# Hybrid decoder layer on one core: the b/a logits with both weight halves in one stationary block, and two banks of activations turned per job

## The reference, cut to what matters

```python
h = rms_norm(x, norm1_g[l])
proj = h @ w_in[l]
qkv_g, z, b_logit, a_logit, q_s, k_s, v_s, gate_logits = jnp.split(proj, split_points, axis=-1)
...
beta = jax.nn.sigmoid(b_logit)
g = -jnp.exp(a_log) * jax.nn.softplus(a_logit + dt_bias)
...
x = x + (g_gdn * y_gdn + g_swa * y_swa) @ w_out[l]
h = rms_norm(x, norm2_g[l])
x = x + jnp.square(jax.nn.relu(h @ w_ff_up[l])) @ w_ff_down[l]
return rms_norm(x, final_norm_g)
```

## Time and profile before

| | before |
|---|---|
| median of 3 runs | 1839.65 us (1839.18 to 1839.65) |
| profiled execution | 1839.5 us |
| its span, first to last instruction | 1837.7 us |
| PE busy | 1818.1 us, 99% of the span, 10928 matmuls |
| PEld busy | 1479.4 us, 81% |
| DVE busy | 1086.0 us, 59% |
| ACT busy | 883.4 us, 48% |
| POOL busy | 115.4 us, 6% |
| DMA, mean over the span | 172 GB/s |

### The profile page before, as it was taken

The page is one execution under the profiler, slowest core; times in us unless marked ns, Lnnn a source line. Parts: engine busy times, 40 slices in busy tenths (PEclk is TensorE's granted clock), DMA queues, the critical chain, the costliest instruction groups (busy, mean ns, idle before and its releaser), DMA issues.

```text
span 1837.7 us, 29585 instructions
## 1 busy us (share of the span) xinstructions
PE 1818.1 (99%) x10928; PEld 1479.4 (81%) x10928; DVE 1086.0 (59%) x1531; ACT 883.4 (48%) x1388; POOL 115.4 (6%) x82
## 2 busy tenths in 40 slices
PE   7999999999999999999999999999999999999998
PEld 6888787787787877778888888888888888888886
DVE  5567686777766576665555555555544455555454
ACT  6464454554644555555444455444433344444443
POOL 0022031040220000000000000000000000000110
PEclk9999999999999999999999999999999999999999
DMA  6543443434434544445656655555555555555554
GB/s 252 173 160 124 142 145 120 150 127 139 149 127 139 182 152 152 151 158 161 205 194 200 206 199 189 188 185 183 193 192 193 192 192 184 185 187 187 194 195 138
DMA packets 88020, 316.33 MB, mean 172 GB/s; under 512 B 9712, under 2 KB 10224, under 8 KB 87792
## 3 DMA queue, kind: packets, MB, share of 16 engines
q1 hardware_dynamic: 87056, 312.58, 50.9%
q0 software_dynamic: 576, 2.10, 0.3%
q10 hardware_dynamic: 288, 0.18, 0.1%
HBM read 312.72 MB, written 2.10 MB: 171 GB/s over the span
## 4 chain that ended last, share of the span: by engine, by line
PE 98%; DVE 0%; issue 0%; DMA 0%; ACT 0%; DVEq 0%; POOLq 0%; POOL 0%; SPq 0%; ACTq 0%
PE acc L325 30%; PE acc L326 29%; PE acc L327 29%; PE J L382 2%; PE J L421 1%; PE J L531 1%; PE J L413 1%; PE J L580 1%; PE J L591 1%; PE J L425 1%; PE J L389 1%; PE J L370 1%; PE J L544 1%; PE J L451 0%; PE J L554 0%
## 5 line engine op out<-in xcount | busy, mean ns | idle before, releaser
L1159 DVE TENSOR_TENSOR w_lo<-raw,w_hi 128x1024 fp32r<-128x1024 f32 x584 | 715.7, 1231 | 506.8 <-ACT w_hi L780 506.1
L780 ACT ACTIVATE w_hi<-raw 128x1024 fp32r<-128x1024 f32 x584 | 617.0, 1060 | 605.4 <-PE acc L327 602.7
L325 PE MATMUL acc<-w_hi,hT_hi 128*128 128x512 f32 x1440 | 579.8, 403 | 5.8 <-DVE hT_lo L1177 4.2
L326 PE MATMUL acc<-w_lo,hT_hi 128*128 128x512 f32 x1440 | 562.8, 391 | 0.0
L327 PE MATMUL acc<-w_hi,hT_lo 128*128 128x512 f32 x1440 | 562.3, 391 | 0.0
L325 PEld LDWEIGHTS acc<-w_hi,hT_hi 128*128 128x128 f32 x1440 | 270.8, 188 | 72.7 <-issue 11.2
L327 PEld LDWEIGHTS acc<-w_hi,hT_lo 128*128 128x128 f32 x1440 | 270.9, 188 | 58.1
L326 PEld LDWEIGHTS acc<-w_lo,hT_hi 128*128 128x128 f32 x1440 | 271.3, 188 | 52.1 <-issue 1.0
L325 PE MATMUL acc<-w_hi,act_hi 128*128 128x512 f32 x512 | 199.3, 389 | 0.0
L327 PE MATMUL acc<-w_hi,act_lo 128*128 128x512 f32 x512 | 199.2, 389 | 0.0
L326 PE MATMUL acc<-w_lo,act_hi 128*128 128x512 f32 x512 | 199.2, 389 | 0.0
(11 more groups left out here) (231 smaller groups left out, 1446.0 us busy)
## 6 DMA issues: line engine op xcount, KB each, us to landing
raw<-weights SPq DMA_DIRECT2D x584, 512.0 KB, 3.3
xres<-x SPq DMA_DIRECT2D x4, 512.0 KB, 7.3
xres<-x POOLq DMA_DIRECT2D x4, 512.0 KB, 5.8
y<-nat SPq DMA_DIRECT2D x8, 256.0 KB, 3.1
fgain_sb<-fgain SPq DMA_DIRECT2D x1, 1024.0 KB, 5.6
masks_sb<-masks SPq DMA_DIRECT2D x1, 576.0 KB, 10.7
zs<-w_ba SPq DMA_DIRECT2D x1, 256.0 KB, 9.2
dist_sb<-dist SPq DMA_DIRECT2D x1, 192.0 KB, 3.3
```

Source lines behind the costliest of these rows:

```text
L325: mm(o, aT_hi[:, kt, tok], w_hi[:, c % RING, w], start=first, stop=False)
L326: mm(o, aT_hi[:, kt, tok], w_lo[:, c % RING, w], start=False, stop=False)
L780: A(w_hi[:, slot], raw[:, slot], ACT.Copy).then_inc(hi_ready, 1)
L1159: tt(w_lo[:, slot], raw[:, slot], w_hi[:, slot].bitcast(F32), ALU.subtract).then_inc(lo_ready, 1)
```

## The change

Four edits belong together in the first part. The tiles `wba_hi` and `wba_lo` become one tile `wba` in which the 32 high and 32 low columns of a channel tile stand side by side; ACT and DVE write it in pieces of 32 columns. The logits' product becomes two matmuls per channel tile with a stationary block of 128 x 64 in place of three with 128 x 32. It also computes low activations by low weights, which was left out before. The result lies on 64 partitions: the part from the high weights on 0 to 31, the part from the low weights on 32 to 63. The copy to `baT` takes 64 partitions. The two transposes at h = 21 become four float32 matmuls with an identity of 64 rows, two accumulating ones per token tile, which turn both parts and add them.

In the second part TensorE's `turn_last` turns both of its banks at h = 4 and `turn_pair` both at h = 6. ACT's and DVE's lists stay as they are.

```diff
--- before.py
+++ after.py
@@ -122,8 +122,7 @@
 
 
         with ExitStack() as first:
-            wba_hi = sb("wba_hi", [P, NB], F32R, first)
-            wba_lo = sb("wba_lo", [P, NB], F32R, first)
+            wba = sb("wba", [P, 2 * NB], F32R, first)
         with ExitStack() as mixers:
             og_hi = sb("og_hi", [P, KT, T], F32R, mixers)
             og_lo = sb("og_lo", [P, KT, T], F32R, mixers)
@@ -211,9 +210,10 @@
         cTu = cT[:].rearrange("p h (t e) -> p (h t) e", t=NT)
 
         nat1 = rawg[:].rearrange("p a t n -> p (a t n)").rearrange("p (t d) -> p t d", t=NT)
-        w_ba_sb = zs[:].rearrange("p h t -> p (h t)")[:, 0:512]
+        wba_hi, wba_lo = (wba[:].rearrange("p (k a n) -> p k a n", a=2, n=32)[:, :, i] for i in range(2))
+        w_ba_sb = zs[:].rearrange("p h t -> p (h t)")[:, 0:512].rearrange("p (k n) -> p k n", n=32)
         ba = vb[:].rearrange("p t n -> p (t n)")
-        baT = kn[0:32, 0, 0:T]
+        baT = kn[0:64, 0, 0:T]
         kdup = rawg[:, 0]
 
         def mat(i):
@@ -287,7 +287,7 @@
             for i in range(4):
                 sp.dma_start(xres[:, :, i * NB:(i + 1) * NB], x[:, :, i * NB:(i + 1) * NB]).then_inc(x_in[i], 16)
                 sp.dma_start(raw[:, i], weights[i]).then_inc(raw_in[i], 16)
-            sp.dma_start(w_ba_sb, w_ba).then_inc(params_in, 16)
+            sp.dma_start(w_ba_sb, w_ba.rearrange("p (k n) -> p k n", n=32)).then_inc(params_in, 16)
             sp.dma_start(rowp[:], rowp_d).then_inc(params_in, 16)
             sp.dma_start(masks[:, P:], masks_d[:, P:]).then_inc(params_in, 16)
 
@@ -611,17 +611,18 @@
                     pe.wait_ge(params_in, 48)
                     pe.wait_ge(wba_ready, 2)
                     for kt in range(KT):
-                        w = slice(kt * 32, (kt + 1) * 32)
-                        o = J[0:32, 1, 0:T]
-                        mm(o, wba_hi[:, w], hT_hi[:, kt, :], start=(kt == 0), stop=False)
-                        mm(o, wba_lo[:, w], hT_hi[:, kt, :], start=False, stop=False)
-                        ins = mm(o, wba_hi[:, w], hT_lo[:, kt, :], start=False, stop=(kt == KT - 1))
+                        w = slice(kt * 64, (kt + 1) * 64)
+                        o = J[0:64, 1, 0:T]
+                        mm(o, wba[:, w], hT_hi[:, kt, :], start=(kt == 0), stop=False)
+                        ins = mm(o, wba[:, w], hT_lo[:, kt, :], start=False, stop=(kt == KT - 1))
                     ins.then_inc(ba_done, 1)
                 if h == 21:
 
                     pe.wait_ge(baT_ready, 1)
                     for t in range(NT):
-                        ins = tr(J[:, 0, t * 32:(t + 1) * 32], baT[:, t * P:(t + 1) * P], ident[0:32, 0:32])
+                        for i in range(2):
+                            ins = mm(J[:, 0, t * 32:(t + 1) * 32], baT[:, t * P:(t + 1) * P], eye64[0:64, i * 32:(i + 1) * 32],
+                                     start=(i == 0), stop=(i == 1))
                     ins.then_inc(ba_T, 1)
                 if h == 32:
 
@@ -642,17 +643,19 @@
             def turn_last(k, filled, value):
 
                 def job(h):
-                    if h == 4 or h == 6:
+                    if h == 4:
                         pe.wait_ge(filled, value)
-                        bank(k, 6 + (h - 4) // 2, xres)
+                        for b in range(2):
+                            bank(k, 6 + b, xres)
                 return job
 
             def turn_pair(k, j, filled, value):
 
                 def job(h):
-                    if h == 6 or h == 10:
+                    if h == 6:
                         pe.wait_ge(filled, value)
-                        bank(k, 2 * j + (h - 6) // 4, xres)
+                        for b in range(2):
+                            bank(k, 2 * j + b, xres)
                 return job
 
             def window(w, jobs, fine):
@@ -977,7 +980,7 @@
                     A(nat1[:, t, w], xres[:, t, w], ACT.Square, accum_out=part[:, t, i:i + 1]).then_inc(ssq_x, 1)
                 if h == 17:
                     act.wait_ge(params_in, 48)
-                    A(wba_hi[:], w_ba_sb, ACT.Copy).then_inc(wba_ready, 1)
+                    A(wba_hi, w_ba_sb, ACT.Copy).then_inc(wba_ready, 1)
                 if h == 22:
 
                     act.wait_ge(ba_link, 1)
@@ -1431,10 +1434,10 @@
                     row_sums(0)
                 if h == 17:
                     dve.wait_ge(wba_ready, 1)
-                    tt(wba_lo[:], w_ba_sb, wba_hi[:].bitcast(F32), ALU.subtract).then_inc(wba_ready, 1)
+                    tt(wba_lo, w_ba_sb, wba_hi.bitcast(F32), ALU.subtract).then_inc(wba_ready, 1)
                 if h == 20:
                     dve.wait_ge(ba_done, 1)
-                    V.tensor_copy(baT, J[0:32, 1, 0:T]).then_inc(baT_ready, 1)
+                    V.tensor_copy(baT, J[0:64, 1, 0:T]).then_inc(baT_ready, 1)
                 if h == 22:
                     dve.wait_ge(ba_T, 1)
                     for t in range(NT):
```

## The result

The changed kernel takes 1847.87 us (median of 6 runs, 1847.04 to 1848.08) against 1839.65 us before: 1.0042 of the time before, 95% interval 1.003 to 1.0054. It is 8.2 us slower, where I had forecast 1.85 us less, and it lies outside the stated range of 1836.6 to 1840.6 us. Its profiled execution took 1848.08 us with a span of 1846.3 us, 8.6 us more than the span before.

What follows compares the result with a forecast made beforehand. The prediction took TensorE's queue to bound the kernel, with no idle time to fill. Logits -1.82, turning at h = 21 +0.69 and merged jobs -0.72 gave -1.85 us, so 1837.8 us, range 1836.6 to 1840.6 us.

Steps and rivals of the forecast that it cites:

- What bounds the kernel: TensorE's queue, PE standing on 98% of the span: the change can only shorten or lengthen what that queue takes.
- The waits of rows 2: PE's profiled waits, 4.2 us for first turned activations, 1.5 us for low weights: neither in a stretch the change touches.
- Part 1a: Logits' product at h = 19: 16 of 48 matmuls go, 0.1138 us each, gain 1.82 us, no cost for wider blocks.
- Parts 1b and 1c: ACT's and DVE's writes in pieces of 32 columns, and DVE's copy of the product on twice the partitions: cost nothing.
- Part 1d: Turning at h = 21: eight float32 passes at 0.115 us replace two transposes, +0.69 us.
- Part 2: Two banks per job in `turn_pair` and `turn_last`: eight merges save 0.09 us each, 0.72 us, with no new wait.
- The sum: All terms together: -1.82 + 0.69 - 0.72 = -1.85 us, predicting 1837.8 us, 0.10% less.
- The series of loads and matmuls: Loads and matmuls in series at h = 19 and 21: +10.5 us, chance 0.04; only at h = 21, +0.9 us, 0.09.
- The clock did fall: Rival: eight transposes in a row lower the clock for twelve main matmuls per doubled job, 19 us slower, chance 0.01.
- the 0.06 for slower: Chance of a slower kernel: 0.04 for full series, 0.01 for the clock, and a little.
- a time outside the range: Sign for the whole kernel: outside 1836.6 to 1840.6 us, something not in TensorE's own queue has moved.

## Why the prediction was wrong, point by point

- *What bounds the kernel.* Right that TensorE's queue is the time, wrong that the change can only lengthen or shorten it by what its own steps take. The place of the unchanged loop in the instruction stream had a price as well, and the prediction put it at nothing without a reason.
- *The waits of rows 2.* I dismissed 1.5 us "in two pieces for low weights" as lying in no stretch that the change touches by a wait. That was the step that failed: the same two waits became 8.2 us, and with the low clock behind them they cost 10.4 us more than before. I never asked where they stood. At 235.51 and 359.72 us, right behind the two jumps, each of 4.5 to 4.6 us on TensorE's sequencer, they were the visible end of a fetch of which nearly all was covered. The writing-out of the loop showed that they had nothing to do with `w_lo`.
- *Part 1a.* Right: 0.1138 us each, no cost for the wider blocks, no drain. A load of 64 columns appears as 0.13 to 0.14 us and lies beside the matmuls.
- *Parts 1b and 1c.* Right: DVE's write in pieces ends as before, and no PE wait appears at h = 19 or 21.
- *Part 1d.* Eight passes as counted, at (51.70 - 50.70) / 8 = 0.125 us rather than 0.115, so +0.77 us where +0.69 stood. The term was a little too small.
- *Part 2.* Right. The job above gives 2 x 0.49 - 0.90 = 0.08 us, and over all eight merges the lag between the two kernels' main matmuls shrinks by 0.69 us, 0.09 each; no new wait.
- *The sum.* Right for the same work placed well: 1838.02 us with one instruction more, against 1837.8. What was missing was +10.4 us at two jumps (3.25 + 1.6 + 3.36 + 2.2). That a queue 20 instructions shorter put the loop's head there was bad luck and nothing in the new work.
- *Rivals.* The series of loads and matmuls did not occur. The clock did fall, but behind an idle stretch, not behind transposes. The loss came from a mechanism that no rival named, and the 0.06 for slower had no share for it. The trace of before had the 4.5 us row of the jump, with idle time behind it, which could have warned of it, but not told on which side of a boundary the change would put the loop's head. I had said that a time outside the range would mean that something outside TensorE's own queue had moved; it was inside it.

By the count the loop's head lies 20 - 1 = 19 instructions behind a boundary in the kernel before; nothing in the code puts it there on purpose. Of the 4.6 us of the jump after, about 2.2 pass before the packet starts, 0.9 while it moves and 1.5 until the next instruction runs. What fills the first and the last part stays open.

## What to carry to other kernels

Where one engine is the bound and its queue has loops whose bodies are longer than what the engine keeps of its instructions, look at each jump of that engine: the duration of its branch, the idle time of the engine just behind it, what the profile gives as its releaser, and the instruction packets in the DMA view. A change of even a few instructions ahead of such a loop moves its head against the block boundaries; time the change also with one or some tens of idle instructions ahead of the loop before judging it. If the program may be longer, write that loop out.

## What the runs showed of the hardware that I had not expected

The jump back of the loop over windows 1 to 3 occupies TensorE's sequencer for 4.45 to 4.84 us over the eight kernels here that have it, while a shorter loop's jump in the same kernel takes 0.23 (the attention loop, L710; the last of the three doesn't jump). One pass of the first has some 2,400 instructions, one of the second some 640, and no q8 packet moves between 746 and 858 us:

```profile
L710 PEldq COMPARE_BRANCH  x3: 83/229/233, 746.5 to 857.3; - x3
```

With 1 instruction of the loop body ahead of the boundary the engine was idle 3.94 and 4.23 us at the two jumps, and the lower clock level behind them cost 1.6 and 2.2 us; with 17 ahead it was idle 0.86 and 0.68 us at the first jump and the clock stayed; with 37 ahead no second wait was left. A wait that the profile names after the last releaser it knows can be the engine's own fetch of instructions.
